# Two down projections in another order: the first group's last tile behind four tiles of the second group

## The reference, cut to what matters

```python
def conv_ffn(x, w_up, conv_w, conv_b, w_down):
    """Gated MLP with a causal depthwise conv (width CONV_W) after the up-projection."""
    h = x @ w_up
    L = h.shape[1]
    hp = jnp.pad(h, ((0, 0), (CONV_W - 1, 0), (0, 0)))
    hc = conv_b
    for j in range(CONV_W):
        hc = hc + hp[:, j:j + L] * conv_w[j]
    u, g = jnp.split(hc, 2, axis=-1)
    return (jax.nn.silu(g) * u) @ w_down
...
for i in range(DEPTH):
    ...
    h = h + conv_ffn(rms_norm(h, ffn_norm[i]), w_up[i], conv_w[i], conv_b[i], w_down[i])
```

## Time and profile before

| what | value |
|---|---|
| time, median of 3 runs | 2265.24 us (2265.05 to 2266.51) |
| time of the profiled execution | 2267.38 us |
| its span in the trace | 2266.1 us |
| mean granted TensorE clock | 0.997 of full speed |
| PE busy | 2241.7 us (99%) |
| DVE busy | 1411.8 us (62%) |
| ACT busy | 1049.8 us (46%) |

### The profile page before, as it was taken

The page is one execution under the profiler, slowest core; times in us unless marked ns, Lnnn a source line. Parts: engine busy times, 40 slices in busy tenths (PEclk is TensorE's granted clock), DMA queues, the critical chain, the costliest instruction groups (busy, mean ns, idle before and its releaser), DMA issues.

```text
span 2266.1 us, 39364 instructions
## 1 busy us (share of the span) xinstructions
PE 2241.7 (99%) x15807; PEld 2027.3 (89%) x15807; DVE 1411.8 (62%) x2601; ACT 1049.8 (46%) x1963; POOL 118.2 (5%) x203
## 2 busy tenths in 40 slices
PE   9999999999999999999999999999999999999998
PEld 7798999999997898999899788977899888898997
DVE  5356576759743465667689566868554465853663
ACT  5356554447533365544377443223244444552652
POOL 3001000000000001100000010101000000000001
PEclk9999999999999999999999999999999999999999
DMA  6545666245433335632365262667711122443551
GB/s 215 167 123 151 179 188 186 100 139 174 134 95 125 113 117 149 181 113 96 109 175 166 81 172 84 190 188 210 201 64 66 66 93 93 149 160 112 183 166 51
DMA packets 97112, 313.01 MB, mean 138 GB/s; under 512 B 13809, under 2 KB 17811, under 8 KB 95907
## 3 DMA queue, kind: packets, MB, share of 16 engines
q1 hardware_dynamic: 84627, 220.93, 29.1%
q0 software_dynamic: 11584, 88.25, 16.6%
q10 hardware_dynamic: 720, 1.31, 0.2%
HBM read 308.32 MB, written 86.02 MB: 174 GB/s over the span
## 4 chain that ended last, share of the span: by engine, by line
PE 92%; DVE 4%; ACT 2%; issue 1%; DMA 0%; POOL 0%; SPq 0%; ACTq 0%; DVEq 0%; POOLq 0%
PE G L1391 58%; PE G L1428 14%; PE G L1501 7%; PE X L1428 2%; DVE wL L2387 1%; PE X L1713 1%; PE X L1795 1%; PE X L1668 1%; PE X L1691 1%; PE X L1779 1%; PE X L1496 1%; ACT wH L1848 1%; PE X L1764 1%; PE X L1391 1%; PE X L1751 0%
## 5 line engine op out<-in xcount | busy, mean ns | idle before, releaser
L1848 ACT ACTIVATE wH<-raw 128x512 fp32r<-128x512 f32 (+3 forms) x693 | 475.0, 704 | 473.9 <-PE G L1391 392.9
L2387 DVE TENSOR_TENSOR wL<-raw,wH 128x512 fp32r<-128x512 f32 (+3 forms) x693 | 538.2, 788 | 240.0 <-ACT wH L1848 236.5
L1391 PE MATMUL G<-aH,wH 128*128 128x264 f32 (+2 forms) x2000 | 503.9, 317 | 2.4 <-DVE aL L2400 1.9
L1391 PE MATMUL G<-aL,wH 128*128 128x264 f32 (+2 forms) x2000 | 481.7, 306 | 0.0
L1391 PE MATMUL G<-aH,wL 128*128 128x264 f32 (+2 forms) x2000 | 481.6, 306 | 0.0
L1391 PEld LDWEIGHTS G<-aH,wH 128*128 128x128 f32 x2000 | 324.4, 189 | 28.9 <-issue 6.1
L1391 PEld LDWEIGHTS G<-aH,wL 128*128 128x128 f32 x2000 | 322.5, 188 | 17.2
L1391 PEld LDWEIGHTS G<-aL,wH 128*128 128x128 f32 x2000 | 322.9, 188 | 14.3 <-issue 0.2
L1428 PE MATMUL G<-seven,wH 128*128 128x256 f32 (+2 forms) x960 | 177.5, 284 | 1.6 <-DVE wL L2387 1.5
L2546 DVE TENSOR_TENSOR hT<-G,hT 128x528 f32<-128x528 f32 (+1 forms) x83 | 58.0, 698 | 188.6 <-PE G L1391 188.6
L1428 PEld LDWEIGHTS G<-seven,wH 128*128 128x128 f32 x960 | 148.0, 188 | 3.8 <-issue 3.0
(11 more groups left out here) (407 smaller groups left out, 3915.0 us busy)
## 6 DMA issues: line engine op xcount, KB each, us to landing
raw<-weights SPq DMA_DIRECT2D x195, 512.0 KB, 3.6
weight_sums<-weights POOLq DMA_DIRECT2D x72, 704.0 KB, 6.3
raw<-weight_sums SPq DMA_DIRECT2D x160, 256.0 KB, 2.8
raw<-weights SPq DMA_DIRECT2D x48, 704.0 KB, 4.1
raw<-weights SPq DMA_DIRECT2D x121, 256.0 KB, 2.7
weight_sums<-weight_sums POOLq DMA_DIRECT2D x24, 704.0 KB, 4.8
weight_sums<-weights POOLq DMA_DIRECT2D x24, 448.0 KB, 4.9
raw<-weights SPq DMA_DIRECT2D x12, 384.0 KB, 6.1
```

What stands on the lines that cost most here:

```text
L1391: done = e.matmul(m.pair(i)[0:M, bank, 0:n], a[:, k, 0:M], b[:, kx, lo - t0:lo - t0 + n], start=(k == 0 and c == 0), stop=(k == nk - 1 and ...
L1848: e.activation(m.high(i)[:, c], m.raw(i)[:, c], ACT.Copy).then_inc(s.w_hi, 1)
L2387: e.tensor_tensor(m.low(i)[:, c], m.raw(i)[:, c], m.high(i)[:, c].bitcast(F32), ALU.subtract).then_inc(s.w_lo, 1)
```

## The change

There are two edits, and both act in the second half of the feed-forward part of layers 0 and 1 only.

In `seven()`, at the last but one product of the half, one chain step is released ahead of the splits, where before the splits came first. One more follows behind them as before. So two steps of hidden tile 9 are released there, its SiLU and its gate product.

A new generator `first_down()` runs the first two down groups of the half. It places tiles 0 to 9 of the first group, tiles 0 to 3 of the second, the last tile of the first, its addition to `hT`, the split of the third group, and then tiles 4 to 10 of the second.

```diff
@@ seven()
-            for what in splits_at(i):
+            splits = splits_at(i)
+            if (half, jj, p) == (1, 10, 3) and f < 2:
+
+                step(*pieces.popleft())
+            for what in splits:
                 step(*what)
@@
+    def first_down():
+
+
+        i = take()
+        n = PLAN[i][0][3]
+        for k in range(n - 1):
+            step("mm", i, k, k + 1)
+            yield
+        drain()
+        j = state["next"]
+        state["next"] += 1
+        background(j)
+        for k in range(4):
+            step("mm", j, k, k + 1)
+            yield
+        step("mm", i, n - 1, n)
+        held.append(i)
+        let_go()
+        splits = splits_at(j)
+        todo.extend(splits + [("rest", i, 0)])
+        rests.clear()
+        drain()
+        for k in range(4, n):
+            step("mm", j, k, k + 1)
+            if k < n - 1:
+                yield
+        held.append(j)
+        let_go()
+        yield
@@ ffn_conv()
-                for j in range(8):
+                if half:
+                    yield from first_down()
+                for j in range(2 * half, 8):
                     yield from fm(before=made[j] if j < len(made) else {})
```

## The result

| | before | the change |
|---|---|---|
| median of 8 runs | 2265.43 us | 2259.26 us |
| lowest and highest | 2265.05 to 2266.70 | 2258.90 to 2259.68 |
| profiled execution (span) | 2267.38 us (2266.1) | 2259.09 us (2257.8) |

The ratio is 0.9972, with a 95% interval of 0.9963 to 0.998: 6.2 us or 0.27% less. The forecast was 2258.0 us, in a range of 2256.7 to 2261.0.

The account below looks back on a forecast made before the run. PE, busy 99% of the span, was taken as the bound. Gaps of 3.98 us plus 3.28 us behind them, 7.26 us, taken from the median 2265.24 gave 2258.0 us, range 2256.7 to 2261.0.

Parts of the forecast that it names:

- Where PE waits, and on what: Last K tile of the first down group waits for `hidL` of hidden tile 10: idle 1.76 us (layer 0), 1.89 (layer 1).
- The stretches at full speed: First to third down group without gaps or slow clock: 16.07 us instead of 19.60 (layer 0), 15.32 instead of 19.05 (layer 1).
- the bound of 0.6 us: Changes between two open PSUM banks: taken as 0, at most 0.6 us in all, three per layer at 0.1 us.
- The gate edit: In `seven()`, gate product ahead of the weight piece: tile 10's chain 0.75 us sooner, counted at nothing because slack hides it.
- What is late next: Third group's weights are the tight point, but ready in time: 1.83 us to spare in layer 0, 1.58 in layer 1.
- the 3.29 us: Time from the first down group's end until the third group's weights are ready in its place.
- the rival on the slower side: Late raw weights make PE wait 2.3 and 2.5 us at the third group, with slow spells: 2266.0 us; chance 0.03.
- The slow spells: Clock falls to about half behind both gaps; taken as gone with the gaps, worth 3.28 us with restarts.
- the clock falls all the same: Rival: only the gaps go, the slow spells stay, 3.98 us won, 2261.3 us; chance 0.08.
- 1.61 for restart and slow spell: Layer 0, behind the gap: 1.61 us of the 3.53 us to be won there.
- 1.67 behind it: Layer 1, behind the gap: 1.67 us of the 3.73 us to be won there.
- The sum: 3.98 us for gaps plus 3.28 behind them, 7.26 us in all, taken from the median of 2265.24: 2258.0 us.

Follow-up runs that it names:

- eight tiles: The change with eight tiles of the second group instead of four in front of the moved tile: 2262.61 us (11 runs).
- the second trace of before: The unaltered kernel before, profiled once more: 2264.27 us, with both gaps and one slow spell, in layer 1.
- the first series: Gate edit alone, moved tile alone, filled gaps and eight tiles, on one chip beside 31 runs of the kernel before, whose median was 2265.66 us.
- first two comparisons: The unaltered change against the kernel before: 2259.26 us against 2265.43, then 2259.19 against 2265.70 beside the longer gaps.
- the third, 2259.80: The unaltered change, beside the moved tile alone and the kernel before (median 2265.18 us): 2259.80 us (11 runs).

## Why the prediction was right, and the term that was too large

*Where PE waits, and on what.* Right: both waits on `hidL` went, and with either edit undone the traces moved as worked out.

*The stretches at full speed.* Right to within 0.02 us: 16.07 and 15.34 us, forecast 16.07 and 15.32. Moving between two open banks costs nothing; the bound of 0.6 us was not needed.

*The gate edit.* Its 0.75 us are there in VectorE's timeline (0.91 in layer 0, 0.96 in layer 1) and lie inside the slack of the moved tile, so they are worth nothing. Alone, it takes the gaps from 1.8 to 0.9 us and wins 3.4 us.

*What is late next.* Right: the third group's weights, with 1.82 and 1.57 us to spare (1.83 and 1.58 forecast), and with eight tiles the waits that the 3.29 us give. This was the rival on the slower side, and its mechanism is real. In the first halves, where VectorE has no idle time between the operand steps, it took 4.4 us.

*The slow spells.* The cause was right: they go with the gaps, and they also go when PE is kept busy in the gaps. That refutes the rival "the clock falls all the same". One reading was off by a little: the longest wait of PE beside the two is not the 1.5 us one but 1.6 us ahead of the very first matmul. The Trainium skill's rule ("TensorE: Matmul & The Clock Gate", "Why this matters for your kernels") let the clock hold through idle gaps longer than these, and the traces do not agree: behind 1.76 and 1.89 us it fell in one execution, and behind 1.81, but not behind 1.76, in the next.

The size was wrong, and this is the term of the sum that failed: "1.61 for restart and slow spell" and "1.67 behind it", 3.28 us in all. They were read from one execution that has both spells in full, about 1.5 us each, with 0.1 us for each restart. With the gaps filled, the kernel is 1.5 us under the median of before. That is the price of one spell, so a middling run seems to have one of the two, as the second trace of before has. The 2.14 us by which the profiled execution lay over the median were in view, and I carried them along as a constant. They were mostly this term: a part of the runs does not pay it.

*The sum.* Within the first series it closes: 3.98 us for the gaps, 0.2 for the restarts and 1.5 for the spells are 5.7, and the moved tile alone is 5.7 us under before. The change gained 6.2 and 6.5 us in its first two comparisons and 5.4 in the third, so the 0.5 to 0.8 us beyond that did not come back and are no effect of the edit that the runs show. Where they came from is open. The time up to the place of the change varies by more: in eleven traces the first down group of layer 0's second half began between 592.45 and 594.58 us, in kernels that have the same program until shortly before that point.

With 5.7 us off 2265.43 the change would be at 2259.7 us. That the first median of 2259.26 came out inside the narrower bounds of 2256.8 to 2259.3 is partly luck; the third, 2259.80, lies outside them and inside the full range.

## What to carry to other kernels

Where a tensor engine waits for the last link of a chain, put work of another accumulation group in front of the wait, and then look at who has lost slack by it: here the weights that replace the group which now ends later. A stall can cost more than its length, through the clock; what it costs on top must be taken from several runs, since one profile shows only one outcome. When the profiled execution lies well over the median, ask which term of the sum makes the difference before subtracting it as a constant.

## What the runs showed of the hardware that was not expected

- The granted clock fell (from 2.4 to 1.2 GHz) behind an idle gap of 1.8 us in some executions and not in others of the same kernel, at the same place. In the fourteen traces, PE has seven gaps of 1.76 to 2.21 us, and the clock fell behind five of them (1.76, 1.81, 1.89, 1.98 and 2.21) and not behind two (1.76 and 2.03). It fell behind none of 1.71 us or less, the last ten microseconds left out, in which PE comes to its end. Each fall came 0.3 to 1.5 us after the restart; its price is about 1.5 us (19.60 against 18.08 us in layer 0 of one and the same kernel).
- The mean clock was 0.999 in all 11 runs of the kernel with two gaps of 0.9 us, and in 19 of the 83 runs of the kernel with two gaps of 1.8 us.
- Matmuls whose result nobody reads, put into the wait, brought the mean clock to 0.999 in all 11 runs, made the kernel 1.5 us faster in the median (interval of the ratio 0.9985 to 1.0002) and narrowed its runs from 4.2 to 1.4 us.
- Leaving an accumulation open in one PSUM bank for four tiles of another group, and coming back to it, cost nothing: 0.73 us per tile throughout in layer 0.
